# Block 2's neighbourhood attention: query tiles of two grid rows against all 512 keys, or of 8 rows by 16 columns against a band of 256

## The reference, cut to what matters

```python
D_MODEL, SEQ, GRID_W, CTX_LEN, N_HEADS, HEAD_DIM = 1024, 512, 64, 256, 8, 64
NA_ROWS, NA_COLS = 8, 16

# each query sees all 8 rows, and in each a window of 16 columns:
c0 = clip(q_col - NA_COLS // 2, 0, GRID_W - NA_COLS)       # keys c0 .. c0+15
d_row, d_col = key_row - q_row + 7, clip(key_col - q_col + 15, 0, 30)
s_loc = q . k + rpb[head, d_row, d_col]                    # -1e30 outside of the window
s_ctx = q . k_ctx                                          # 256 context keys, no bias
p = softmax(concat(s_loc, s_ctx)); o = p_loc @ v + p_ctx @ v_ctx
x = x + g1 * (concat([y_conv, y_attn]) @ w_out)
```

## Time and profile before

| | |
|---|---|
| median of the three runs shown | 3074.81 us (3072.08 to 3076.34) |
| span of the profiled execution | 3089.8 us; no other time of that execution is shown |
| busy in the span | PE 88%, DVE 30%, ACT 15%, POOL 16% |
| attention, 1885.5 to 2033.1 us of the span | 147.6 us |
| then until the experts' router is done, to 2096.3 | 63.2 us |
| granted TensorE clock, mean of the span | 0.952 |

### The profile page before, as it was taken

How to read it: one execution, slowest core, us unless ns; L and a number is a source line. 1 busy time by engine, 2 the same in 40 slices (tenths; PEclk the granted TensorE clock), 3 DMA queues, 4 the chain that set the end, 5 groups by cost and what they waited for, 6 DMA issues and landing times.

```text
span 3089.8 us, 37118 instructions
## 1 busy us (share of the span) xinstructions
PE 2710.8 (88%) x15553; PEld 1335.5 (43%) x15553; DVE 925.4 (30%) x1555; ACT 456.3 (15%) x999; POOL 505.8 (16%) x384
## 2 busy tenths in 40 slices
PE   7998799999999899989998697795988898888887
PEld 4545567744455554444544333443322233233232
DVE  2045456530244211111111595733111211111112
ACT  2013233210031111111111202520000000000001
POOL 0002243320010334333443102200000000000000
PEclk9999899999998999999999798897999999999999
DMA  5110355332125799989997311036999999999997
GB/s 227 55 55 0 119 182 190 115 157 82 55 87 190 259 389 377 376 302 388 375 363 263 154 55 36 12 137 247 427 428 427 428 427 428 427 427 428 428 427 308
DMA packets 99532, 792.24 MB, mean 256 GB/s; under 512 B 18962, under 2 KB 19346, under 8 KB 53288
## 3 DMA queue, kind: packets, MB, share of 16 engines
q1 hardware_dynamic: 74440, 743.66, 59.0%
q0 software_dynamic: 23088, 37.82, 5.0%
q10 hardware_dynamic: 1840, 8.40, 0.7%
HBM read 768.48 MB, written 38.86 MB: 261 GB/s over the span
## 4 chain that ended last, share of the span: by engine, by line
PE 60%; DMA 25%; DVE 9%; issue 3%; ACT 2%; POOL 1%; SPq 0%; POOLq 0%; ACTq 0%; DVEq 0%
DMA arena<-in_w_down 13%; PE b L3110 10%; DMA yd<-arena 7%; PE b L1539 5%; PE b L1980 5%; PE b L553 4%; DMA arena<-h2d,arena 3%; PE b L1994 3%; PE b L555 3%; PE b L3150 3%; PE b L2577 3%; PE b L3125 2%; PE b L1606 2%; PE b L1557 2%; DVE arena L2623 2%
## 5 line engine op out<-in xcount | busy, mean ns | idle before, releaser
L3110 PE MATMUL b<-arena 128*64 128x512 f32 x2048 | 456.8, 604 | 24.8 <-DMA arena<-in_w_up 12.6
L1980 PE MATMUL b<-arena 128*64 128x256 f32 x3072 | 355.8, 384 | 3.9 <-DMA arena<-in_w_gu 2.7
L3110 PEld LDWEIGHTS b<-arena 128*64 128x64 f32 x2048 | 154.4, 138 | 321.3 <-issue 283.0
L3125 PE MATMUL b<-arena 128*64 128x512 f32 x1024 | 232.4, 597 | 62.1 <-DMA arena<-in_w_down 50.5
L1980 PEld LDWEIGHTS b<-arena 128*64 128x64 f32 x3072 | 213.1, 137 | 115.7 <-issue 5.0
L2296 POOL DMA_INDIRECT yd<-arena x96 | 152.2, 1586 | 337.1 <-ACT arena L2078 127.4
L1994 PE MATMUL b<-arena 128*64 128x512 f32 x768 | 187.3, 608 | 0.7 <-issue 0.7
L2253 DVE TENSOR_TENSOR arena<-arena,b 128x128 f32<-128x128 f32 x96 | 27.8, 290 | 517.8 <-ACT arena L2071 486.8
L3125 PEld LDWEIGHTS b<-arena 128*64 128x64 f32 x1024 | 71.2, 136 | 221.8 <-issue 114.6
L3248 DVE TENSOR_TENSOR arena<-arena,b 128x512 f32<-128x512 f32 x32 | 20.6, 686 | 479.1 <-PE b L3110 479.1
L1539 PE MATMUL b<-arena 128*128 128x512 f32 x370 | 159.4, 592 | 0.8 <-DVE arena L1361 0.8
(11 more groups left out here) (500 smaller groups left out, 3331.3 us busy)
## 6 DMA issues: line engine op xcount, KB each, us to landing
arena<-in_w_gu SPq DMA_DIRECT2D x65, 2048.0 KB, 10.3
arena<-in_w_gate SPq DMA_DIRECT2D x64, 2048.0 KB, 30.5
arena<-in_w_up SPq DMA_DIRECT2D x64, 2048.0 KB, 30.0
arena<-in_w_down SPq DMA_DIRECT2D x63, 2048.0 KB, 25.3
arena<-in_w_dn SPq DMA_DIRECT2D x65, 1024.0 KB, 13.9
arena<-in_w_mod SPq DMA_DIRECT2D x80, 512.0 KB, 4.3
arena<-in_w_in SPq DMA_DIRECT2D x18, 2048.0 KB, 8.6
arena<-yd SPq DMA_DIRECT2D x12, 512.0 KB, 8.6
```

Source lines behind the costliest of these rows:

```text
L1980: x = e.matmul(ps[i % 2][64 * j:64 * j + 64, 0:256], XGT[i % 2][:, k % 4, (k // 4) * 64:(k // 4) * 64 + 64], GUB[place_of(w)][:, k, j * 25 ...
L3110: x = e.matmul(ps[b + c][64 * hf:64 * hf + 64, :], XS[q % 2][:, kb, (n % 2) * 64:(n % 2) * 64 + 64], w[:, at_w:at_w + 512], start=(kb == 0 ...
L3125: x = e.matmul(p[64 * hf:64 * hf + 64, :], H[:, c * 4 + j, hi * 64:hi * 64 + 64], w[:, i * 1024 + hf * 512:i * 1024 + hf * 512 + 512], sta ...
```

## The change

It alters the attention of block 2 and what prepares it, and nothing else.

- **Tiles.** A tile is now 8 rows by 16 columns of the grid for one pair of heads (c = n // 4, b = n % 4). Its queries see only 32 columns, that is 256 keys (`BANDS`), and the 256 context keys. So that a band is one piece, ACT writes queries and keys of `projections2` in an order of 8 groups of 8 columns (`by_rows`, `by_groups`).
- **Scores.** One bank per head and tile takes both parts: columns 0 to 255 the band, 256 to 511 the context. Two banks per head take turns. The bias and mask go into the bank by a product of the identity with `RPB` (128x256), as the last of the tile's six products of 256 columns.
- **Softmax.** DVE takes the maximum straight from the bank (two of 512). ACT takes the exponential straight from the bank (two of 512). DVE's bias additions and ACT's copy of the context's scores are gone. The scaling is two of 128x512.
- **Transposes and values.** 8 transposes per tile into banks 4 and 5, one copy of 128x512 each on ACT and DVE. The values are 8 products of 128 columns per tile, two tiles later. They need the values' rows by pairs of groups (`VP`, seven tiles of 128x512): `projections2` writes `VT` to memory (`vd`, 4 transfers on SP) and POOL gathers it back by 7 indirect transfers with the row numbers `pairs`.
- **Other.** `RPB` is 128x768 per head, the mask is a table of 128x768 that comes by DMA first, and POOL's adding of it runs on 768 columns. `w_out_2` is asked for behind the first four `RPB`. ACT's SiLU sits at n = 12.

```diff
+BANDS = (0, 1, 3, 4)
+KINDS = (0, 1, 1, 2)
...
@@ projections2
+        for t in range(4):
+            e.wait_ge(*act_.at("out", number["v", t]))
+            e.dma_start(K.vd[t * 128:(t + 1) * 128, :], VT[:, t, :]).then_inc(*kept_v.up("values", t))
...
-                e.activation(KF[:, where, :], p[:, :], ACT.Copy).then_inc(*act_.up("out", i))
+                e.activation(by_groups(KF[:, where, :]), by_rows(p[:, :]), ACT.Copy).then_inc(*act_.up("out", i))
...
+        e.wait_ge(*came_pairs.at("pairs"))
+        e.wait_ge(*kept_v.at("values", 3))
+        rows.done(e)
+        for g in range(7):
+            e.indirect_dma_start(K.VP[g], None, K.vd, off(pairs.bitcast(U32)[:, g:g + 1])).then_inc(*K.came_vp.up("pair", g))
...
@@ attention: sp
+        e.dma_start(mask, I["valid_2"]).then_inc(*came_m.up("bands"))
+        for c in range(4):
+            if c >= 2:
+                e.wait_ge(*mm.at("scores", 4 * (c - 2) + 3))
+            for h in (2 * c, 2 * c + 1):
+                e.dma_start(RPB[h % 4], I["rpb_2"][h].rearrange("p (v n) -> p v n", v=3)).then_inc(*came_r[h % 4].up(h))
+            if c == 1:
                 for i in range(2):
                     e.dma_start(wo[i], I["w_out_2"][i]).then_inc(*came_wo[i].up())
...
@@ attention: pe
+        for n in range(N + 2):
+            if n < N:
+                scores(e, n)
+            if n < 2:
+                ym(e, 2 * n)
+                ym(e, 2 * n + 1)
+            if n >= 2:
+                values(e, n - 2)
+            if 1 <= n <= N:
+                spread(e, n - 1)
...
     def scores(e, n):
+        if n >= 2:
+            e.wait_ge(*act_.at("exp", n - 2, 1))
+        for i in range(2):
+            r = slice(64 * i, 64 * i + 64)
+            e.matmul(score(n, i)[:, 0:256], QF[r, c, hs(b)], KF[r, c, at_k:at_k + 256], start=True, stop=False, skip_group_check=True)
+        for i in range(2):
+            r = slice(64 * i, 64 * i + 64)
+            e.matmul(score(n, i)[:, 256:512], QF[r, c, hs(b)], KFc[r, c, :], start=False, stop=False, skip_group_check=True)
+        for i in range(2):
+            h = 2 * c + i
+            e.wait_ge(*pool_.at("valid", h))
+            x = e.matmul(score(n, i)[:, 0:256], K.ident, RPB[h % 4][:, KINDS[b], :], start=False, stop=True, skip_group_check=True)
+        x.then_inc(*mm.up("scores", n))
...
     def values(e, n):
+        e.wait_ge(*act_.at("pt", n))
+        e.wait_ge(*dve.at("pt", n))
+        if n == 0:
+            e.wait_ge(*K.came_vp.at("pair", 6))
...
@@ attention: act
+            if n >= 2:
+                e.wait_ge(*mm.at("spread", n - 2, 0))
+                if n >= 4:
+                    e.wait_ge(*mm.at("values", n - 4))
+                e.activation(PT[n % 2][:, 0, :, :], heads(ps[4][:, :]), ACT.Copy).then_inc(*act_.up("pt", n - 2))
+            if n < N:
+                if n >= 2:
+                    e.wait_ge(*mm.at("spread", n - 2, 1))
                 e.wait_ge(*dve.at("max", n))
+                    e.activation(SB[n % 2][:, i, :], score(n, i)[:, :], ACT.Exp, bias=mx[:, j:j + 1],
...
@@ attention: dve_
+            if n >= 2:
+                e.wait_ge(*mm.at("spread", n - 2, 1))
+                e.tensor_copy(PT[n % 2][:, 1, :, :], heads(ps[5][:, :])).then_inc(*dve.up("pt", n - 2))
+            if 1 <= n <= N:
+                e.wait_ge(*act_.at("exp", n - 1, 1))
+                e.reciprocal(z, z).then_inc(*dve.up("z", n - 1))
+                    e.tensor_scalar(p, p, z[:, i:i + 1], None, ALU.mult).then_inc(*dve.up("p", n - 1))
+            if n < N:
+                e.wait_ge(*mm.at("scores", n))
+                    e.tensor_reduce(mx[:, 2 * n + i:2 * n + i + 1], score(n, i)[:, :], AX, ALU.max).then_inc(*dve.up("top", n, i))
+                e.tensor_scalar(m_, m_, -1.0, None, ALU.mult).then_inc(*dve.up("max", n))
```

More of the change, by code:

```diff
@@ L2515, in projections2 @@
     K.VC, K.CY, K.YCT, K.YAT = VC, CY, YCT, YAT = fm(542), fm(512), fm(512), fm(512)
-    K.RPB = [ar(896).rearrange("p (m n) -> p m n", m=14) for _ in range(2)]
+    K.RPB = [ar(768), ar(768)]
+    ar(256)
     cw = fm(32)
@@ L2520, in projections2 @@
     K.keep5 = ar.at
+    K.VP = [VT[:, g, :] for g in range(4)] + [gain[:, 0:512], gain[:, 512:1024], K.arena[:, K.keep5 + 11264:K.keep5 + 11776]]
+    pairs = K.tiny(7).bitcast(I32)
+    came_pairs, kept_v, K.came_vp = S.dma("convw"), S.dma("wrt"), S.dma("xg0")
     wr = [ar(4096), ar(4096), K.area(K.keep1 + 12504)(4096)]
@@ L2654, in attention @@
     K.att = (mm, dve, act_, pool_)
-    PARTS = (((0, 0, 4),), ((0, 4, 2), (1, 0, 2)), ((1, 2, 4),))
-    on_dve = lambda part, n: part == 0 or (part == 2 and n % 2 == 1)
+    N = 16
+    tile_of = lambda n: (n // 4, n % 4)
+    score = lambda n, i: ps[2 * (n % 2) + i]
     def sp(e):
         all_of(e, *K.proj2)
-        for c in range(5):
-            if c == 4:
-                e.wait_ge(*mm.at("values", 2, 5))
+        e.dma_start(mask, I["valid_2"]).then_inc(*came_m.up("bands"))
[5 more added lines that the diff above has]
+            if c == 1:
@@ L2730, in spread @@
         if n:
[L2731 to L2732 removed]
+            e.wait_ge(*act_.at("pt", n - 1))
+            e.wait_ge(*dve.at("pt", n - 1))
+        for i in range(2):
             for k in range(4):
[L2734 to L2740 removed]
@@ L2770, in act @@
+                x = e.matmul(ps[6 + c % 2][64 * i:64 * i + 64, hs(b)], v[:, h * 64:(h + 1) * 64], PT[n % 2][:, i, k, :],
+                             start=(k == 0), stop=(k == 3), skip_group_check=True)
+        x.then_inc(*mm.up("values", n))
     def act(e):
         all_of(e, *K.proj2)
-        for n in range(20):
-            if n < 16:
+        for n in range(N + 2):
+            if n < 2:
+                for t in (2 * n, 2 * n + 1):
+                    e.wait_ge(*mm.at("ym", t))
+                    e.activation(YM[:, t, :], ps[6 + t % 2][:, :], ACT.Copy).then_inc(*act_.up("ym", t))
+            if n >= 2:
[4 more added lines that the diff above has]
+            if n < N:
@@ L2826, in dve_ @@
[L2826 to L2833 removed]
+            if n == 1:
                 e.wait_ge(*act_.at("ym", 3))
                 e.tensor_reduce(m4, YM, AX, ALU.add).then_inc(*dve.up("sum"))
[L2836 removed]
```

216 lines of the change are left out of this document (80 added, 136 removed).

## The result

| | before | changed kernel |
|---|---|---|
| median | 3075.51 us (3072.08 to 3076.34, 4 runs) | 3042.45 us (3031.31 to 3053.14, 4 runs) |
| the same, in a later comparison | 3075.34 us (3070.28 to 3081.76, 9 runs) | 3037.83 us (3036.92 to 3038.55, 4 runs) |
| profiled execution, time | not shown | 3038.84 us |
| its span | 3089.8 us | 3037.2 us |
| attention | 147.6 us | 107.4 us |

The ratio of the changed kernel to the one before is 0.9883, with a 95% interval of 0.985 to 0.9915: 26 to 46 us faster, 36 in the middle. The later comparison gave 0.9877 (0.9861 to 0.9893), 33 to 43 us. Forecast were 40.4 us and a time of 3034.

The account below looks back on a forecast made before the run. A ring of waits over ACT and DVE was taken to bound the attention, whose end starts the experts' weight stream. Terms -37.4 + 3 + 1.5 + 0.3 - 7.8 = -40.4 took 3074.8 to 3034 us, range 3024 to 3052.

Parts of the forecast that it names:

- Ring: Attention's loop of waits between ACT and DVE: 6.55 to 4.06 us per tile, -37.4 us over 15 tiles.
- Disturbances: Attention time outside the steady tiles: POOL holding up DVE +3 us, PE at the lower clock +1.5.
- Start: Attention's start until the first exponential, with mask and bias loads: +0.3 us, bounds -1.5 and +3.
- End: From the last tile's first exponential to the attention's end: 14.8 us becomes 7, -7.8 us.
- PE, 3.7 us a tile: PE's products and transposes per attention tile: 3.7 us, just below the ring, so PE nearly full.
- Rival B: PE becomes the attention's ring if small pairs don't overlap: 4.6 to 5.3 us a tile, 3043 to 3053; chance 0.12.
- C: PE stays at 1.2 GHz in the attention: 7.4 us a tile, gain 8.5, 3066 us; chance 0.06.
- D: PE at 1.2 GHz and no pair overlapping: 10.5 us a tile, +40 us, 3115 us; chance 0.03.
- The port: SBUF port shared by DVE and POOL: three instructions per tile could each lose one of POOL's, upper bound +22 us.
- Stages behind, nothing: The two stages after the attention stay at 63 and 993 us; copies and gathers there cost nothing, copies at most +0.6.
- E: Slack in the experts' weight stream hides the attention's gain, so the end stays at 3075 us; chance 0.04.

Follow-up runs that it names:

- e2: Changed kernel with the identity product removed and DVE adding the bias in the bank before its maxima: 3052.4 us, attention 119.2, steady tile 4.86.
- e6: Changed kernel with every tile's scores in the same pair of banks: 3055.43 us, attention 124.8, steady tile 5.32.
- e1: Changed kernel with POOL's layer norm on 8 columns per token in place of 512, variance a maximum: 3033.4 us, attention 97.3.
- e5: Changed kernel with mask and first four bias tables fetched and added during the projections: median 3033.73 us, ratio 0.9875 to the kernel before.
- e4: Changed kernel with DVE's maxima and negation of a tile ahead of earlier tiles' copy, inversion and scaling: 3071.25 us, attention 135.9, steady tile 6.53.
- e9: e8 with the transposes of the convolution's output ahead of the next scores in the first two iterations: median 3023.6 us, ratio 0.9836 to the kernel before.
- e4 and e5: Changed kernel with the edits of e4 and e5 together: 3069.89 us, attention 129.1, steady tile 6.52.
- e8: Changed kernel with the edits of e7 and e5 together: 3034.76 us, attention 99.5, steady tile 4.18.
- e7: Changed kernel with e4's order on DVE and PE issuing scores a tile ahead: 3044.67 us, attention 109.4, steady tile 4.18.

## Why the prediction was right, and where its steps were off

- **Ring, -37.4.** Measured 6.55 to 4.06, exactly the sum, but that it is exact is luck, since two of its terms were off by 0.06 and cancelled: exponentials until the inversion 1.48 and not 1.54, negation until the next exponential 0.26 and not 0.20. That ACT's copy and DVE's copy are hidden holds. e2 (+0.80 a tile) and e6 (scores in the ring, 5.32) show by two edits that this ring sets the steady tile.
- **Disturbances, +4.5.** From the first exponential to that of tile 15 it is 1973.83 - 1886.08 = 87.75 us, of which 15 x 4.06 = 60.9 is ring. 26.85 are left where 22.7 were: +4.2. In it, POOL's stalls rose by 6.4 us (18.7 in place of 12.3; I had said 13 to 18, so a little over), of which I had put +3 on the path. e1 shows that the layer norm's share of the stalls, 12.7 us of waiting, costs 10.1 us of stage. At that rate 6.4 us of waiting are some 5 us (an estimate), more than the +3, and the rest came out near -1 where +1.5 was put for the low clock: the mean granted clock rose from 0.81 to 0.92. So the sum of this term is right partly by luck. What the clock did by itself was not separated.
- **Start, +0.3.** Measured +1.0: POOL's first two additions ended and the identity products ran at 1881.2, 7.7 us after the first issue at 1873.5, and the negation was done at 1884.7, but ACT was still copying two transposed pieces of the convolution and loading a table (1.28 us) until 1886.1, which I had left out. e5 puts the price of the whole wait for the bias at 7.3 us of start, and 5.0 or 7.4 of stage in its two profiles.
- **End, -7.8.** Measured -7.9.
- **PE, 3.7 us a tile.** This was the step that was mis-sized: 4.18. Values 1.03 and transposes 1.02 were near (1.0 and 0.97). Band and context took 1.07 and not 0.86, and the identity's products 1.06 and not 0.86. The trace shows where: inside a group the starts of the single instructions are 0.21 to 0.22 us apart, as the sum had it (context 1970.55 and 1970.77; identity 1971.40, 1971.62, 1971.83), but 0.31 to 0.32 at the last step of a group and the first of the next where the shape of the weights changes, from 64x128 to 128x128 to 128x64 (1970.77 to 1971.08 and to 1971.40, then 1971.83 to 1972.14; band 1970.01 to 1970.33). Four such steps of 0.1 are the 0.4 that were missing. The change from band to context, with one shape, has none. "Just below the ring" was really just above it, by 0.12. It cost little: a ring of 4.06 and an engine of 4.18 differ by 15 x 0.12 = 1.8 us at most. In e1, where POOL is out of the way, the late tiles come at PE's 4.18. Rival B (4.6 to 5.3) had the right mechanism, and its condition failed: the small pairs do overlap, 16 instructions of the values in 1.03 us.
- **Clock (C, D).** The mean granted clock is 0.92 and not 0.5. It fell behind PE's long waits: eight transposes after waits of 5.96 and 3.29 us lasted 1.97, those after waits of 1.93 us and less 1.09. Between them it was chance: behind a wait of 2.65 us ahead of tile 14 the granted clock stayed at 1.00 in both profiles of the changed kernel and in one of e5, and was low in the other of e5 and in e1, at 1.4 to 1.6 us of that interval. At the start a wait of 4.67 us for the bias had the same effect (1.92). "TensorE: Matmul & The Clock Gate" of the Trainium skill, Part 1, says that idling lowers the clock, and the traces agree. Its Part 4, by which transposes do not count as activity in the way that products do, had made me give C its chance; here a quarter of PE's work is transposes, and in the tiles without a wait the full clock held.
- **The port.** "SBUF — State Buffer" of the Trainium skill, section "SBUF: two separate sides", has an exclusive lock held for a whole instruction. The traces agree instruction by instruction: scalings of 3.27 and 4.73 us, which take 0.45 alone, each ended 0.3 us behind an instruction of POOL. What the prediction drew from it, that three instructions of each tile could each lose one of POOL's and the sum end nearer the upper bound of +22, did not come: the trace gives +6.4 of waiting, since each of the layer norm's instructions held up at most one of DVE's.
- **Stages behind, nothing.** Measured 63.2 and 993.3, as before (E falls). The reordering copies last 0.66 and not 0.60 us, and only the last is uncovered. The gathers were issued from 1820.3 to 1829.3, over 60 us ahead of the first values at 1893.1.

The sum by the measured parts is -37.35 + 4.15 + 1.0 - 7.9 = -40.1 in the stage, against -40.4. The medians differ by 33.1 and 37.5 us, the ratios give 36 and 38, and both intervals hold 40.4. The forecast of 3034 is 4 to 8 us below the two medians; what ran ahead of the attention varies by as much.

## What to carry to other kernels

An order written out by hand is one order over all engines. Changing it on one (e4) cost 28 us; the same edit with PE's list and the place of the small side jobs changed to match (e9) took 8.5 us off the attention of e5. Before moving an instruction, follow who waits for what stood ahead of it, round to itself. And a side job on POOL that looks hidden is not, if its instructions hold up those of the ring's engine: here 12.7 us of waits were worth 10.

## What the hardware showed that I had not expected

- POOL's instructions hold DVE one by one or all together, by what DVE is doing. Scalings (one input) get in between two of POOL's: two of 0.45 us took 7.01 us across two of the layer norm's, 8.86 in e9, and 3.78 across two additions of the mask without a gap (1908.76 to 1912.54), of which the second then lasted 1.98 and not 1.81. A tap of the convolution (two inputs) sat through all four additions of the mask, 7.67 us in place of 0.75, and so it did in both profiles of e5, in "e4 and e5", e8 and e9. That the number of inputs makes the difference was not tried.
- A PE engine that waits 7.3 us pays twice: 7.3 for the wait, and then half speed for about four microseconds (1944.3 to 1948.5 in e7).
- Products that mix widths are dearer than the pairs of 512 columns tell: 8 instructions of 256 columns in pairs take 1.07 us, not the 0.86 of a half of the earlier trace rows, and the 4 that use the whole array 1.06. The 0.1 us more lies at each step around a change of the weights' shape. No edit tried a list with fewer such changes.
